# VectorE adds its half of a row one step sooner, and a seventh row buffer, in a mixture-of-experts and transformer kernel on one core

## The chip, the cores and the metric

The kernel runs on one core of a Trainium2 chip. The metric is the device time of one launch in microseconds. Three timed runs of the kernel before gave 3349.99, 3354.9 and 3366.16 us, median 3354.9. The engines are TensorE (PE, its weight loads PEld), VectorE (DVE), ScalarE (ACT), GpSimd (POOL) and SyncE (SP), which only issues transfers.

## What is computed

512 tokens of width 1024 in fp32 go through two blocks. The part that matters here is the end of the first block, a feed-forward layer that picks for every token 128 of 16384 experts (8 heads, 16 each), and the second block, which follows it:

```python
best, pos = lax.top_k(cand.reshape(...), 16)
gate = jax.nn.softmax(best, axis=-1)
ue = jnp.take(expert_u, expert, axis=0)
ve = jnp.take(expert_v, expert, axis=0)
h = jax.nn.gelu(jnp.einsum('thkd,td->thk', ue, xc))
out = jnp.einsum('thk,thkd->td', gate * h, ve)
```

Then come a final norm and the second block: differential attention, an MLP with squared ReLU (width 4096), multi-head latent attention (MLA), the same MLP with other weights, and a norm.

## The kernel before, in words

Each engine runs one long program in the order in which its instructions were written, and waits on semaphores for the others.

**Rows.** The tokens are four tiles of 128. For tile tt and choice k there is one "row", n = 128 tt + k, so 512 rows. For row n GpSimd issues one indirect transfer (`pool_rows`, L1708) that brings for each of the 128 tokens the 2048 values (u and v) of its k-th expert into a row buffer of 128 x 2048 values. VectorE then takes the dot product of the u half with the normed tokens (`dve_dot`, L1826). ScalarE makes from it the row's weight (`act_weight`: gelu L1776, times the gate L1778) and a diagonal matrix of the weights (L1783). The v half times the weight is added up in PSUM. For rows 0 to 255 TensorE does this for all 1024 columns, by a matmul with the diagonal (`pe_rows`, L1727). For rows 256 to 511 (`both_add`) TensorE adds columns 0 to 511 and VectorE adds columns 512 to 1023 (`dve_rows`, L1808; the first row of a tile L1805). The row buffer is free when both have added.

**Buffers.** `row_of(n)` gives the buffer of row n. Rows below 236 use ten buffers, later rows six (numbers 4 to 9: two in `un`, four in `raw`), since the others' place is taken by split weights of the tail. `row_before(n)` is the row that had the buffer before, and the gather of row n waits for the adds of that row. The normed tokens lie in `XN`, four tiles of 1024 columns. From row 256 on the dot product reads them from PSUM instead, where ScalarE copies tile 2 at step 255 and tile 3 at step 383 (L1757). `sums` are two places for the finished sum of a tile (`act_join`, L1792); sums[1] is filled at row 255, read by the transposes right after, and next filled at row 511.

**Steps.** All engines go through rows by steps. At step s VectorE does dot(s+1) and then the add of `late(s)`, which is s below 256 and s-1 (`LAG` = 1) from 256 on; ScalarE makes the weight of s+1; TensorE adds `late(s)`.

**The tail beside the rows.** The tail is the second block, and it runs for each half of the tokens. Steps 256 to 512 run beside the tail of the first half: `with_rows` and `beside` put 1.1 steps (`RATE`) after each unit of tail work, in the same places on every engine. The second half's tail then runs alone. The tail's weights come from HBM in tiles of 512 KB that SyncE loads (`sp_load`, L283), four raw places in turn. ScalarE rounds a tile to a high part (`act_hi`, L292), GpSimd subtracts it to get the low part (`pool_lo`, L298), and TensorE works with both.

**GpSimd's order.** GpSimd has gathers and splits to do. `self.spot` holds the place on TensorE, counted in turns, at which a row is added or a weight tile is used last. Before the gather of row n, `pool_rows` puts all the splits whose place came free on TensorE no later than the buffer of row n did. So the distance of six rows sets both what a gather waits for and where it stands among the splits.

The functions touched are `peer_tiles` (from L1363), `row_of`, `pool_rows`, `act_rows` and `dve_rows`.

Of the kernel before, what the change touches and what calls it, by code (L numbers as in the profile page):

```python
# [18 lines left out]
NBANK = 8  # L19
FEW_ROWS = 236  # L20
RATE = 1.1
LAG = 1
COLS = 53120
A_U = 5504
# [2 lines left out]
A_W2 = A_RAW + 8192  # L27
A_T = A_W2 + 8192
A_G = A_T + 8192
A_GEL = A_G + 4096  # L30
# [157 lines left out]
class Net:  # L188
# [1174 lines left out]
    def peer_tiles(self):  # L1363
        U, scr = 4096, self.scr
# [24 lines left out]
        self.modw = self.raw[0:4]  # L1389
        un = self.un  # L1390
        self.rows = [self.w01[:, 2048 * i:2048 * i + 2048] for i in range(4)] + [un[:, 0:2048], un[:, 2048:4096]] + self.raw[0:4]
        self.chosen = [un[:, 4096 + 128 * i:4224 + 128 * i].bitcast(U32) for i in range(4)]
        self.gate = [un[:, 4608 + 128 * i:4736 + 128 * i] for i in range(4)]
        self.dots, self.gelus, self.weight = (un[:, 5120 + 128 * i:5248 + 128 * i] for i in range(3))
# [4 lines left out]
    @staticmethod  # L1399
    def row_of(n):  # L1400

        return n % 10 if n < FEW_ROWS else 4 + (n - FEW_ROWS) % 6

    def row_before(self, n):

# [281 lines left out]
    def pool_rows(self, e):  # L1687
        S = "peer_pool"
        lows = [k for k in self.keys if len(k) == 3]
        at = 0  # L1690
        for n in range(512):
            tt, k, r = n // 128, n % 128, self.row_of(n)
            before = self.row_before(n)
            while n >= FEW_ROWS + 12 and at < len(lows) and self.spot_before(lows[at]) <= self.spot.get(("row", before), 0):
                self.pool_lo(e, lows[at])
                at += 1
            if k == 0:
                e.wait_ge(*self.at("peer_dve", ("expert", tt)))
            if before is not None:
                e.wait_ge(*self.at("peer_pe", ("acc", before)))  # L1700
                if self.both_add(before):
                    e.wait_ge(*self.at("peer_dve", ("acc", before)))
            elif r == 0:
                e.wait_ge(*self.at("peer_pe", ("xn", 3, 1)))
            elif r == 6:
                e.wait_ge(*self.at("peer_pe", "mod20"))
            index = bass.IndirectOffsetOnAxis(ap=self.chosen[tt][:, k:k + 1], axis=0)
            e.indirect_dma_start(self.rows[r], None, self.d["peer_uv"], index).then_inc(*self.tick(f"row{r}", n, 16))  # L1708
        for key in lows[at:]:
            self.pool_lo(e, key)  # L1710
# [39 lines left out]
    def act_rows(self, e):  # L1750
        S, D_, P_ = "peer_act", "peer_dve", "peer_pe"
        for n in range(-1, 512 + LAG):
            if n in (255, 383):
                e.wait_ge(*self.at(D_, ("dot", n)))
                if n == 255:
                    e.wait_ge(*self.at(S, ("sums", 0)))
                e.copy(self.xn_bank(), self.XN[:, n // 128 + 1, :]).then_inc(*self.tick(S, ("xn", n // 128 + 1)))  # L1757
            if n + 1 < 512:
                self.act_weight(e, n + 1)
            if self.late(n) in (127, 255, 383, 511):  # L1760
# [32 lines left out]

    def dve_rows(self, e):
        S, A_, P_ = "peer_dve", "peer_act", "peer_pe"
        for step in range(-1, 512 + LAG):
            if step + 1 < 512:
                self.dve_dot(e, step + 1)
            n = self.late(step)
            if n is not None and self.both_add(n):  # L1800
                v, w, acc = self.rows[self.row_of(n)][:, 1536:2048], self.weight[:, n % 128:n % 128 + 1], self.ps[:, 7, :]
                e.wait_ge(*self.at(A_, ("weight", n)))
                if n % 128 == 0:
# [2 lines left out]
                else:  # L1806
                    e.wait_ge(*self.at(S, ("acc", n - 1)))
                    e.scalar_tensor_tensor(out=acc, in0=v, scalar=w, in1=acc, op0=ALU.mult,  # L1808
                                           op1=ALU.add).then_inc(*self.tick(S, ("acc", n)))
            if step in (130, 386 + LAG):  # L1810
                for j in range(8):
                    self.dve_join(e, step // 128 - 1, j)
            yield

    def dve_dot(self, e, n):
# [1239 lines left out]
```

## Time and profile before

| | us |
|---|---|
| median of 3 timed runs | 3354.9 (3349.99 to 3366.16) |
| profiled execution | 3351.66 |
| its span, first to last instruction | 3349.8 |
| TensorE busy | 2778.6 (83%) |
| VectorE busy | 1978.0 (59%) |
| GpSimd busy | 1667.0 (50%) |
| ScalarE busy | 1433.5 (43%) |
| gathers' transfers, share of the 16 DMA engines | 39.8% |

The first block's other parts take until about 760 us. The rows of the first two tiles follow until about 1440 us, with the gathers as the main load. Rows 256 to 511 run with the tail of the first half until about 2550 us, and the second half's tail runs to the end. A busy share over the whole span mixes these. A table by stretches of time shows for each engine its busy time there, the TensorE clock that was granted (1 is 2.4 GHz), the share of the DMA engines and the bytes moved. A table of waits names for each group of instructions the engine or transfer that came last before they could start.

### The profile page before, as it was taken

The numbers are of one execution on the slowest core, as the hardware profiler recorded it, in microseconds if no ns is written. First come the engines' busy times: TensorE is split into PE (matmuls) and PEld (weight loads), VectorE is DVE, ScalarE is ACT, GpSimd is POOL, SyncE is SP. The second block draws the span as 40 slices with busy tenths as digits, with TensorE's granted clock in tenths as the row PEclk, the third lists the DMA queues.
The fourth block names the chain that finished last, engine by engine and source line by source line (L and its number), as shares of the span: only waits on it lengthen the run. The fifth ranks groups of instructions, "written<-read, shape, count | busy, mean of one in ns | idle before, by whom it ended". The sixth has DMA issues, their size and how long they took to land.

```text
span 3349.8 us, 43400 instructions
## 1 busy us (share of the span) xinstructions
PE 2778.6 (83%) x15438; PEld 2137.0 (64%) x15438; DVE 1978.0 (59%) x4260; ACT 1433.5 (43%) x3189; POOL 1667.0 (50%) x1014
## 2 busy tenths in 40 slices
PE   6987997787788787779778987678887989988898
PEld 4846996562333332266467766457776968987898
DVE  5785444466776766676765657666666464245423
ACT  2222222223333333356845445675444344444543
POOL 3812222254444443446257765447774607863575
PEclk8988998898999999888789998889998989988999
DMA  7210001219999999779669997888995404642364
GB/s 286 90 62 1 1 1 51 115 49 405 421 421 421 421 421 421 309 306 383 242 246 354 380 360 275 349 301 336 382 369 224 153 1 146 190 139 75 113 177 126
DMA packets 140518, 797.49 MB, mean 238 GB/s; under 512 B 15504, under 2 KB 18704, under 8 KB 67600
## 3 DMA queue, kind: packets, MB, share of 16 engines
q0 software_dynamic: 73728, 536.90, 39.8%
q1 hardware_dynamic: 65856, 253.36, 22.0%
q10 hardware_dynamic: 720, 4.46, 0.3%
q8 instruction: 124, 2.03, 0.2%
q14 instruction: 90, 0.74, 0.1%
HBM read 788.10 MB, written 6.55 MB: 237 GB/s over the span
## 4 chain that ended last, share of the span: by engine, by line
PE 45%; DMA 14%; DVE 11%; issue 10%; POOL 9%; ACT 5%; ACTq 0%; DVEq 0%; POOLq 0%; SPq 0%
PE ps L1727 7%; PE ps L2435 6%; DMA raw<-in_peer_uv,un 6%; PE ps L1925 6%; PE ps L870 6%; PE ps L2456 6%; DMA w<-in_peer_uv,un 5%; PE ps L328 4%; POOL wls L298 3%; POOL wlw L298 3%; DMA un<-in_peer_uv,un 2%; POOL raw L1708 2%; DVE scratch L1826 2%; PE ps L2122 2%; DVE gel L1985 1%
## 5 line engine op out<-in xcount | busy, mean ns | idle before, releaser
L298 POOL TENSOR_TENSOR wls<-raws,whs 128x1024 fp32r<-128x1024 f32 (+1 forms) x256 | 610.4, 2394 | 423.2 <-ACT whs L292 420.9
L1727 PE MATMUL ps<-raw,un 128*128 128x512 f32 x760 | 405.7, 650 | 109.1 <-ACT un L1783 106.8
L1708 POOL DMA_INDIRECT raw<-in_peer_uv,un x276 | 283.6, 1027 | 311.6 <-PE ps L1727 153.7
L1776 ACT ACTIVATE un<-un 128x1 f32<-128x1 f32 x512 | 103.7, 202 | 717.7 <-DVE scratch L1826 681.0
L1925 PE MATMUL ps<-ts,whs 128*128 128x256 f32 x1424 | 303.4, 314 | 25.0 <-DVE ts L1994 21.5
L298 POOL TENSOR_TENSOR wlw<-raws,whw 128x1024 fp32r<-128x1024 f32 x112 | 267.6, 2404 | 109.6 <-ACT whw L292 109.3
L292 ACT CAST whs<-raws 128x1024 fp32r<-128x1024 f32 (+1 forms) x256 | 263.8, 1036 | 87.3 <-PE ps L2456 35.4
L1727 PEld LDWEIGHTS ps<-raw,un 128*128 128x128 f32 x760 | 137.3, 203 | 253.9 <-ACT un L1783 173.6
L1826 DVE SCALAR_TENSOR_TENSOR scratch<-raw,ps 128x1024 f32<-128x1024 f32 x172 | 209.4, 1217 | 149.7 <-DMA raw<-in_peer_uv,un 145.3
L1925 PEld LDWEIGHTS ps<-ts,whs 128*128 128x128 f32 x1424 | 242.5, 206 | 56.6 <-issue 34.2
L1727 PE MATMUL ps<-w,un 128*128 128x512 f32 x384 | 201.7, 670 | 89.2 <-ACT un L1783 89.2
L1727 PE MATMUL ps<-un 128*128 128x512 f32 x392 | 209.7, 647 | 53.9 <-ACT un L1783 53.7
L2456 PE MATMUL ps<-ts,whs 128*128 128x256 f32 x1216 | 244.6, 302 | 3.2 <-DVE ts L2509 3.2
L1783 ACT ACTIVATE un<-kept,un 128x128 f32<-128x128 f32 x512 | 205.7, 402 | 48.5 <-ACT un L1778 1.5
L1708 POOL DMA_INDIRECT un<-in_peer_uv,un x140 | 136.9, 978 | 164.8 <-PE ps L1727 82.4
L2435 PE MATMUL ps<-ts,whw 128*128 128x256 f32 x960 | 196.0, 305 | 24.7 <-DVE ts L1994 21.7
L2456 PEld LDWEIGHTS ps<-ts,whs 128*128 128x128 f32 x1216 | 196.5, 195 | 25.6 <-issue 20.7
L1925 PE MATMUL ps<-ts,wls 128*128 128x256 f32 x712 | 210.2, 295 | 0.0
L2435 PE MATMUL ps<-ts,whs 128*128 128x256 f32 x1088 | 209.2, 293 | 0.0
L1727 PEld LDWEIGHTS ps<-w,un 128*128 128x128 f32 x384 | 75.9, 210 | 208.6 <-ACT un L1783 137.8
L298 POOL TENSOR_TENSOR wl<-raw,wh 128x2048 fp32r<-128x2048 f32 x23 | 106.9, 4656 | 201.9 <-ACT wh L292 201.9
L1708 POOL DMA_INDIRECT w<-in_peer_uv,un x96 | 102.8, 1070 | 176.9 <-PE ps L1727 152.6
(426 smaller groups left out, 7069.9 us busy)
## 6 DMA issues: line engine op xcount, KB each, us to landing
raws<-in_w_up SPq DMA_DIRECT2D x128, 512.0 KB
raws<-in_w_down SPq DMA_DIRECT2D x128, 512.0 KB
raws<-in_w_qk SPq DMA_DIRECT2D x32, 512.0 KB
scratch<-in_ada_w SPq DMA_DIRECT2D x13, 1024.0 KB, 14.3
raw<-in_w_in SPq DMA_DIRECT2D x11, 1024.0 KB, 5.9
raw<-in_ada_w SPq DMA_DIRECT2D x11, 1024.0 KB, 4.8
raw<-in_peer_w_q SPq DMA_DIRECT2D x8, 1024.0 KB, 7.0
raws<-in_w_v SPq DMA_DIRECT2D x16, 512.0 KB
```

Of the source, the lines that this page charges most:

```text
L292: e.copy(self.wh[h][:, 0:width], self.raw[slot][:, 0:width]).then_inc(*self.tick("hi", key))
L298: e.tensor_tensor(self.wl[h][:, 0:width], self.raw[slot][:, 0:width], self.wh[h][:, 0:width].bitcast(F32), ALU.subtract).then_inc(*self.ti ...
L328: ins = e.matmul(self.ps[:, b, :], l, r, start=k == 0 and i == 0, stop=k == nk - 1 and i == 2)
L870: ins = e.matmul(self.ps[:, b, 128 * q:128 * q + 128], l, r, start=n == 0, stop=n == len(terms) - 1)
L1708: e.indirect_dma_start(self.rows[r], None, self.d["peer_uv"], index).then_inc(*self.tick(f"row{r}", n, 16))
L1727: ins = e.matmul(self.ps[:, b + half, :], self.diag[n % 4], self.rows[self.row_of(n)][:, 1024 + 512 * half:1536 + 512 * half], start=k == ...
L1776: e.activation(self.gelus[:, c], self.dots[:, c], ACT.Gelu, bias=0.0, scale=1.0).then_inc(*self.tick(S))
L1783: e.activation(self.diag[n % 4], self.C("ident"), ACT.Identity, bias=0.0, scale=self.weight[:, c]).then_inc(*self.tick(S, ("diag", n)))
L1826: e.scalar_tensor_tensor(out=self.junk[n % 2 if n < 256 else 1], in0=self.rows[r][:, 0:1024], scalar=1.0, in1=xn, op0=ALU.mult, op1=ALU.mu ...
L1925: ins = e.matmul(o[:, 0:256], l, r, start=k == 0 and i == 0, stop=k == nk - 1 and i == 2)
L2435: ins = e.matmul(o[:, 0:256], l, r, start=k == 0 and n == 0, stop=k == 7 and n == 2)
L2456: ins = e.matmul(o[:, 0:256], l, r, start=t == 0 and n == 0, stop=t == 3 and n == 2)
```

## The change

The change does four things. First, VectorE's loop no longer lags: at step n it does dot(n+1) and then adds row n, not row n-1. TensorE still adds `late(n)`. Second, from row 278 (`SEVEN_ROWS`) on there are seven row buffers; the new one, number 10, is the place of tiles 2 and 3 of `XN`. Third, since that place is needed, ScalarE copies tile 3 of the normed tokens to sums[1] at step 270, after the transposes that read sums[1], and copies it from there to PSUM at step 383. Fourth, the first gather into buffer 10 (row 284) waits for that move.

```diff
--- before.py
+++ after.py
@@ -19,6 +19,7 @@
 NBANK = 8
 FEW_ROWS = 236
 RATE = 1.1
+SEVEN_ROWS = 278
 LAG = 1
 COLS = 53120
 A_U = 5504
@@ -1389,6 +1390,7 @@
         self.modw = self.raw[0:4]
         un = self.un
         self.rows = [self.w01[:, 2048 * i:2048 * i + 2048] for i in range(4)] + [un[:, 0:2048], un[:, 2048:4096]] + self.raw[0:4]
+        self.rows.append(scr[:, A_G - A_W2 + 2048:A_GEL - A_W2])
         self.chosen = [un[:, 4096 + 128 * i:4224 + 128 * i].bitcast(U32) for i in range(4)]
         self.gate = [un[:, 4608 + 128 * i:4736 + 128 * i] for i in range(4)]
         self.dots, self.gelus, self.weight = (un[:, 5120 + 128 * i:5248 + 128 * i] for i in range(3))
@@ -1399,7 +1401,10 @@
     @staticmethod
     def row_of(n):
 
-        return n % 10 if n < FEW_ROWS else 4 + (n - FEW_ROWS) % 6
+
+        if n < FEW_ROWS:
+            return n % 10
+        return 4 + (n - FEW_ROWS) % 6 if n < SEVEN_ROWS else 4 + (n - SEVEN_ROWS) % 7
 
     def row_before(self, n):
 
@@ -1700,6 +1705,8 @@
                 e.wait_ge(*self.at("peer_pe", ("acc", before)))
                 if self.both_add(before):
                     e.wait_ge(*self.at("peer_dve", ("acc", before)))
+            elif r == 10:
+                e.wait_ge(*self.at("peer_act", "xn moved"))
             elif r == 0:
                 e.wait_ge(*self.at("peer_pe", ("xn", 3, 1)))
             elif r == 6:
@@ -1754,7 +1761,12 @@
                 e.wait_ge(*self.at(D_, ("dot", n)))
                 if n == 255:
                     e.wait_ge(*self.at(S, ("sums", 0)))
-                e.copy(self.xn_bank(), self.XN[:, n // 128 + 1, :]).then_inc(*self.tick(S, ("xn", n // 128 + 1)))
+                    e.copy(self.xn_bank(), self.XN[:, 2, :]).then_inc(*self.tick(S, ("xn", 2)))
+                else:
+                    e.copy(self.xn_bank(), self.sums[1]).then_inc(*self.tick(S, ("xn", 3)))
+            if n == SEVEN_ROWS - 8:
+                e.wait_ge(*self.at(P_, ("join", 1, 1)))
+                e.copy(self.sums[1], self.XN[:, 3, :]).then_inc(*self.tick(S, "xn moved"))
             if n + 1 < 512:
                 self.act_weight(e, n + 1)
             if self.late(n) in (127, 255, 383, 511):
@@ -1793,11 +1805,10 @@
 
     def dve_rows(self, e):
         S, A_, P_ = "peer_dve", "peer_act", "peer_pe"
-        for step in range(-1, 512 + LAG):
-            if step + 1 < 512:
-                self.dve_dot(e, step + 1)
-            n = self.late(step)
-            if n is not None and self.both_add(n):
+        for n in range(-1, 512 + LAG):
+            if n + 1 < 512:
+                self.dve_dot(e, n + 1)
+            if 0 <= n < 512 and self.both_add(n):
                 v, w, acc = self.rows[self.row_of(n)][:, 1536:2048], self.weight[:, n % 128:n % 128 + 1], self.ps[:, 7, :]
                 e.wait_ge(*self.at(A_, ("weight", n)))
                 if n % 128 == 0:
@@ -1807,9 +1818,9 @@
                     e.wait_ge(*self.at(S, ("acc", n - 1)))
                     e.scalar_tensor_tensor(out=acc, in0=v, scalar=w, in1=acc, op0=ALU.mult,
                                            op1=ALU.add).then_inc(*self.tick(S, ("acc", n)))
-            if step in (130, 386 + LAG):
+            if n in (130, 386 + LAG):
                 for j in range(8):
-                    self.dve_join(e, step // 128 - 1, j)
+                    self.dve_join(e, n // 128 - 1, j)
             yield
 
     def dve_dot(self, e, n):
```

## Rows read from the trace of the kernel before

**Rows 1.** VectorE's adds, from their line's view; then stretches of time.
```profile
L1808 DVE SCALAR_TENSOR_TENSOR ps<-raw,un,ps x170: 743/751/755, 1446.9 to 2548.6; 128x512 f32<-128x512 f32 x170
...
core 0: us, PE busy (x) PEld busy (x) DVE busy (x) ACT busy (x) POOL busy (x), PEclk, DMA share, GB/s
1530.00:1590.00 60.00, 54.79 (x257) 36.55 (x257) 39.26 (x92) 39.80 (x90) 34.12 (x24) 0.83 0.96 386
1740.00:2036.00 296.00, 261.87 (x1681) 218.77 (x1679) 180.42 (x354) 148.98 (x347) 205.68 (x127) 0.97 0.88 343
2036.00:2290.00 254.00, 184.50 (x897) 134.84 (x898) 177.63 (x368) 166.55 (x371) 126.89 (x91) 0.85 0.85 322
2290.00:2545.00 255.00, 227.52 (x1474) 190.89 (x1472) 153.10 (x297) 127.61 (x298) 189.37 (x116) 0.97 0.93 361
```

**Rows 2.** Waits, 1740 to 2036 us: who for whom, total, times, longest.
```profile
DVE scratch L1826 <- DMA raw<-in_peer_uv,un: 61.5, 35, 4.9
...
DVE scratch L1826 <- DMA un<-in_peer_uv,un: 39.9, 20, 3.7
...
PE ps L1727 <- ACT un L1783: 28.0, 21, 3.0
```

**Rows 3.** Waits, 2290 to 2548 us.
```profile
DVE scratch L1826 <- DMA raw<-in_peer_uv,un: 61.8, 37, 4.4
DVE scratch L1826 <- DMA un<-in_peer_uv,un: 34.5, 18, 3.9
...
PE ps L1727 <- ACT un L1783: 16.7, 18, 3.4
```

**Rows 4.** Timeline of GpSimd in the first MLP: start, duration, instruction, idle before.
```profile
1786.84 2.40 POOL L298 TENSOR_TENSOR wlw<-raws,whw 128x1024 fp32r<-128x1024 f32 x1 [5.91 <-ACT whw L292]
...
1816.21 0.96 POOL L1708 DMA_INDIRECT raw<-in_peer_uv,un  x1
1817.86 0.94 POOL L1708 DMA_INDIRECT raw<-in_peer_uv,un  x1 [0.68 <-issue]
1825.55 2.39 POOL L298 TENSOR_TENSOR wlw<-raws,whw 128x1024 fp32r<-128x1024 f32 x1 [6.75 <-ACT whw L292]
1828.10 0.96 POOL L1708 DMA_INDIRECT un<-in_peer_uv,un  x1 [0.16 <-issue]
...
2010.83 2.41 POOL L298 TENSOR_TENSOR wlw<-raws,whw 128x1024 fp32r<-128x1024 f32 x1 [6.77 <-ACT whw L292]
```

**Rows 5.** DMA view, 1815 to 1851 us, in 40 slots of 0.9 us.
```profile
GB/s 414 414 428 432 419 414 410 419 451 432 437 382 137 0 0 86 218 455 423 428 369 410 150 309 341 296 423 437 423 428 391 460 446 428 391 405 405 432 423 419
```

**Rows 6.** The stretches' table, 1000 to 1100 us, gathers alone.
```profile
1000.00:1100.00 100.00, 79.38 (x183) 31.77 (x181) 71.35 (x217) 35.45 (x116) 44.25 (x41) 0.96 1.01 421
```

**Rows 7.** Waits, 2036 to 2290 us.
```profile
POOL raw L1708 <- DVE ps L1808: 48.1, 15, 4.7
...
PE ps L1727 <- ACT un L1783: 19.9, 11, 2.9
```

**Rows 8.** Timeline, a weight and the next dot product, in MLP and attention.
```profile
1862.02 0.29 ACT L1778 ACTIVATE un<-un 128x1 f32<-128x1 f32 x1
1863.01 1.22 DVE L1826 SCALAR_TENSOR_TENSOR scratch<-un,ps 128x1024 f32<-128x1024 f32 x1
...
2149.79 1.21 DVE L1826 SCALAR_TENSOR_TENSOR scratch<-un,ps 128x1024 f32<-128x1024 f32 x1
...
2153.31 0.30 ACT L1778 ACTIVATE un<-un 128x1 f32<-128x1 f32 x1
```

**Rows 9.** Timeline of ScalarE at row 384.
```profile
2008.81 0.99 ACT L1792 COPY un<-ps 128x1024 f32<-128x1024 f32 x1
```

**Rows 10.** Timeline, a weight load and the cast that needs it.
```profile
1831.53 0.33 SPq L283 DMA_DIRECT2D raws<-in_w_up  x1
...
1837.82 1.05 ACT L292 CAST whw<-raws 128x1024 fp32r<-128x1024 f32 x1
```

## The prediction

> **What bounds the kernel now.** I read the table by stretches first, because the change touches only rows 256 to 511, which share the time from about 1440 to 2550 us with the tail of the first half of the tokens (VectorE's adds start from 1446.9 to 2548.6 us [rows 1]). In it, look at the last columns. In the two MLP stretches [rows 1] TensorE is busy 261.9 of 296 us and 227.5 of 255 us, and the DMA share is 0.88 and 0.93. In the MLA stretch, 2036 to 2290 us, TensorE is at 184.5 of 254 us and DMA at 0.85. No engine is full in any of them, so something waits in a circle, and the next view is who waits for whom.
>
> Look at the MLP stretches: everybody waits for a row that has not landed. VectorE's dot product stands still for a gather 61.5 + 39.9 us in the first [rows 2] and 61.8 + 34.5 us in the second [rows 3]; TensorE waits 28.0 and 16.7 us for the diagonal that follows from that dot product [rows 2, 3]. The question is why the gather is late. It is not for want of a free buffer: GpSimd has no wait of note there for either accumulation. It is GpSimd's order. In its timeline [rows 4] it issues two gathers at 1816.21 and 1817.86, then reaches a split of weights whose high part ScalarE has not made, stands 6.75 us, and issues the next gather at 1828.10. The same stall is seen from 1786.84 to 2010.83 us in each of six spacings of (2010.83 - 1786.84) / 6 = 37.3 us, one group of the MLP (eight weight tiles). What it does to the DMA engines is in the rates of 0.9 us slots from 1815 us [rows 5]: some 420 GB/s before, then 137, 0, 0, 86, 218, then 455. With weights and gathers both held up behind that split, the DMA engines run dry once per group; otherwise they are full. The gathers alone, without weights, run at 421 GB/s [rows 6].
>
> **In the MLA stretch** the picture is another one. GpSimd waits there for VectorE's accumulation, 48.1 us for the raw buffers alone [rows 7], but VectorE's dot products hardly wait for rows; the attention's own round trips set the pace. An earlier gather is worth little there.
>
> **The change part by part.** The sum is made against the profiled execution, 3351.7 us with a span of 3349.8; the median of the three timed runs is 3354.9, which is 3.2 above it.
>
> *Seventh buffer: depth and order.* Row 278 is the first of seven. Each gather now waits for the accumulation seven rows back, not six. And since GpSimd's order is laid out by the place on TensorE at which that earlier row is used, each gather also moves one row ahead in the order, past about one weight split. In the stretch shown, the gather of 1828.10 would stand before the split that stalls until 1825.55, and be issued near 1818.8. So one more gather fills the dip of each group. GpSimd gets no added instruction; a split that the gather passes starts up to 0.96 us later [rows 4], and where it stalls, not at all. It is 128 x 8192 bytes = 1.05 MB, 2.49 us at 421 GB/s [rows 6]. The MLP stretches hold (296 + 255) / 37.3 = 14.8, say 15 groups: 15 x 2.49 = 37.4 us. Two ceilings on it from other rows: the DMA engines' unused time in these stretches, 296 x 0.12 + 255 x 0.07 = 53.4 us [rows 1], and TensorE's waits for the diagonal, 28.0 + 16.7 = 44.7 us [rows 2, 3]. 37.4 is under both; I keep it.
>
> *The same in the other stretches.* From 1530 to 1590 us the DMA share is 0.96 [rows 1], 2.4 us unused: I take 1, between 0 and 2.4. In the MLA stretch TensorE waits 19.9 us for the diagonal [rows 7], mostly behind VectorE's own attention work: I take 2, between 0 and 19.9.
>
> *VectorE's accumulation one step sooner.* The same instructions in a new order: no busy time is added. Before, step n did dot(n+1) then add(n-1); now it does dot(n+1) then add(n), which needs the weight of row n. In the MLP that weight ends at 1862.02 + 0.29 = 1862.31, and dot(n+1) ends at 1864.2 [rows 8], so the add does not wait. Setting every row's weight against the end of the next dot product over rows 257 to 510, it was later in 4 of 254, by 4.1 us in all; the worst is in attention, where the weight ends at 2153.61 and the dot product at 2151.0 [rows 8]. Cost: 0 to 4.1 us, taken as 0, as that engine's waits in attention cover it. Its gain: where GpSimd waits for VectorE's add (attention), the gather goes out a step sooner, onto DMA engines that are not what is late; taken as nothing beyond the 2 above. In the MLP GpSimd does not wait for the add, so alone this part is worth nothing there. On VectorE's queue the add moves past one dot product and past the piece of the tail between two steps; nothing else moves.
>
> *Moved and added on ScalarE.* One copy of 128x1024 at row 270 that was not there. A copy of this size took 0.99 us [rows 9]. ScalarE waits for a dot product at every row in this stage and the transposes it waits for are done long before; 0 to 1 us, taken as 0. The copy at 383 has another source and the same size. The gather of row 284 waits for the copy of step 270; fourteen rows lie between.
>
> *Row 384.* VectorE's add of row 384 moves ahead of dot(386), and it waits for ScalarE's copy of the sums, which runs from 2008.81 to 2009.80 [rows 9]. VectorE would come there about 2 us too early, once, and dot(386) is queued behind it: +2, between 0 and 4.
>
> *Weights against gathers.* The gather that fills the dip stands in front of weight loads. One load is issued at 1831.53 and cast by ScalarE at 1837.82, 6.3 us later [rows 10]; some two loads of a group have as little room. If they land 2.49 us later, ScalarE stands in order, and row weights are queued behind it. From both sides: 0, or 15 x 2 x 2.49 = 75 us if all of it reached TensorE. I take 3, near the lower end, because ScalarE's waits for a weight load are too small in both MLP stretches to be among the rows of note and it idles before nearly every row.
>
> The sum: 3351.7 - 37.4 - 1 - 2 + 2 + 3 = 3316.3 in terms of the profiled execution; against the median, which lies up to 3.2 higher, 3318.
>
> A rule of the Trainium skill speaks against this gain. First the row: gathers alone moved 421 GB/s for 100 us [rows 6], and the MLP stretches move 343 and 361 [rows 1]. The page "DMA: Bandwidth & Descriptors", section "Where 436 GB/s comes from", says that for transfers between HBM and SBUF the HBM side binds at about 358 GB/s per core. By it the MLP stretches would be at their ceiling and the time would stay near 3352. The trace disagrees, with 421 GB/s held for 100 us.
>
> **The rivals.**
> *The queue only gets longer (chance 0.19).* If the DMA engines' real ceiling with two kinds of traffic is near the share they have, an earlier gather lands no earlier. For: slots at full share around the dip vary from 150 to 455 GB/s [rows 5], so mixed traffic is less even than gathers alone. Against: the slots with 0. It would give back at most what the share leaves in the second stretch, 255 x 0.07 = 17.9 us with nothing from the first, less the 5 of costs: about 3339, and down to no change.
> *More than the dip (0.05).* If the circle of waits opens, TensorE's waits for the diagonal go altogether: 44.7 + 19.9 = 64.6 us, 3287.
> *Slower (0.08).* Later weight loads hold ScalarE, which holds the rows' weights, and TensorE waits for both. Price 75 us at the full rate; less the 37.4 it is 3351.7 + 38 = about 3390. It decides when more than half of those delays reach TensorE (2.49 x 30 x 0.5 = 37.4). Against it: 6.3 us is the tightest case I saw, and a load of half a gather's size has to land in that.
> *It does not do what it says.* Possible only if GpSimd's order stayed as it is and only the wait changed; then the MLP keeps its stall and only the MLA stretch gains, 0 to 4 us: counted with the first rival.
>
> **How the numbers follow.** The forecast has 0.68, the rivals as above. What a measurement of this kernel can tell from no change is about 0.5%, 16.8 us: under 3338 is faster, over 3372 slower. Faster: 0.68 + 0.05 = 0.73; same 0.19; slower 0.08. The forecast's own range is 3300 (the DMA ceiling in place of 37.4: 3351.7 - 53.4 - 3 + 5) to 3338; to hold 8 in 10 it is widened to 3296 and, for part of the first rival, to 3349.
>
> **What would show it.** In the profile after: the 37.3 us between once-a-group stalls down to about 34.8; VectorE's waits for rows in the MLP stretches down from 198 us to under 100; DMA share there up to about 0.97; VectorE's last add some 35 us before 2548.6; the second half's tail as long as before. GpSimd should wait for VectorE's add hardly at all, and for TensorE's more. The prediction is wrong if the DMA share rises but the groups stay as long (first rival), or if ScalarE's casts wait for weight loads (the slower case).

## The result, and the profile after

The changed kernel takes 3293.4 us (median; 3289.4 to 3296.3) against 3353.8 for the kernel before in the same series: a ratio of 0.9819, 95% interval 0.9803 to 0.9835, 60 us faster. Of all the executions in this document only two, both of the first experiment's kernel, stood apart, at 5362 and 5486 us; the ratios leave them out. The profiled execution is the fastest one, 3289.4 us with a span of 3287.6, so the two profiles differ by 62.2 us of span. The forecast was 3318 with 3296 as its lower end: the direction was right, the gain was about 1.7 times the 36 us that the forecast stands for, and the time lies just under the range.

Where the 62 us went is read by row numbers, not by equal times, since the later rows now come earlier. I divide both traces at VectorE's dot products of rows 320, 392, 448 and 511: a stretch of the first MLP, the MLA stretch, and one of the second MLP. First the table by stretches of the kernel after, its last line being the second half of the tokens, where no rows are gathered:

```profile
core 0: us, PE busy (x) PEld busy (x) DVE busy (x) ACT busy (x) POOL busy (x), PEclk, DMA share, GB/s
1734.00:2014.50 280.50, 258.84 (x1722) 218.71 (x1720) 195.14 (x378) 157.50 (x367) 215.51 (x133) 0.98 0.94 378
2014.50:2245.30 230.80, 171.29 (x839) 124.05 (x840) 166.38 (x349) 156.94 (x351) 118.75 (x86) 0.88 0.89 340
2245.30:2483.40 238.10, 228.70 (x1527) 193.82 (x1525) 160.15 (x310) 133.68 (x311) 193.04 (x117) 0.99 0.97 392
2540.00:3287.00 747.00, 680.68 (x5149) 654.58 (x5147) 313.60 (x745) 329.66 (x599) 423.90 (x178) 0.94 0.41 125
```

The same rows in the kernel before, divided at the same dot products (the stretches of [rows 1] are of the same kind, divided at round times):

```profile
1731.40:2043.60 312.20, 269.10 (x1723) 224.68 (x1723) 191.90 (x378) 157.07 (x367) 215.67 (x133) 0.96 0.89 346
2043.60:2279.80 236.20, 174.28 (x841) 126.22 (x840) 166.71 (x348) 157.44 (x352) 118.08 (x85) 0.86 0.86 322
2279.80:2544.70 264.90, 235.94 (x1524) 198.11 (x1524) 159.71 (x310) 133.78 (x311) 194.14 (x118) 0.97 0.92 357
2602.00:3349.70 747.70, 681.27 (x5143) 655.40 (x5141) 312.12 (x742) 329.50 (x599) 424.31 (x178) 0.94 0.41 124
```

The reader should see three things. The MLP stretches lose 31.7 and 26.8 us, 58.5 together; the MLA stretch loses 5.4; the second half is unchanged (row 320 itself comes 2.6 us later than before). The numbers of matmuls, splits and casts agree to within a few, so the same work is done. How well one such length repeats is shown by the twelfth experiment below, whose kernel differs from the changed one only in the second half: its three stretches took 281.9, 230.5 and 239.9 us, so a difference of under 2 us between single profiles says nothing. And TensorE gained twice: its idle time fell from 43.1 to 21.7 us and from 29.0 to 9.4 (41.0 together), and its busy time for the same matmuls fell from 269.1 to 258.8 and from 235.9 to 228.7 (17.5 together), with a granted clock that rose from 0.96 and 0.97 to 0.98 and 0.99.

Who waits for whom after, in the first MLP stretch and then in the second (engine, tile and line, what it waits for: us, times, longest), to be set beside [rows 2, 3]:

```profile
DVE scratch L1837 <- DMA raw<-in_peer_uv,un: 40.1, 31, 2.4
POOL wls L299 <- ACT whs L293: 27.2, 11, 12.9
POOL wlw L299 <- ACT whw L293: 24.0, 9, 6.1
...
DVE scratch L1837 <- DMA un<-in_peer_uv,un: 16.1, 12, 2.2
...
PE ps L1734 <- ACT un L1795: 9.1, 12, 1.7
...
PE ps L1734 <- ACT un L1804: 5.4, 1, 5.4
```

```profile
DVE scratch L1837 <- DMA raw<-in_peer_uv,un: 35.2, 29, 2.2
...
DVE scratch L1837 <- DMA un<-in_peer_uv,un: 18.0, 15, 2.3
...
PE ps L1734 <- ACT un L1795: 4.1, 5, 1.2
```

(L1837 is the dot product, L1826 before; L1734 the accumulation, L1727 before; L1795 the diagonal, L1783 before; L1804 the copy of a finished sum, L1792 before; L299 the split, L298 before; L293 ScalarE's cast, L292 before.) TensorE's waits for the diagonal are down from 28.0 and 16.7 us to 9.1 and 4.1. GpSimd's waits for a cast are down too. In the kernel before they were, in the first stretch:

```profile
POOL wls L298 <- ACT whs L292: 44.1, 13, 12.5
...
POOL wlw L298 <- ACT whw L292: 34.5, 11, 6.8
```

That is 78.6 us, and 51.2 after; in the second stretch 59.7 became 35.9. GpSimd's order, from its timeline after (start, duration, instruction, idle before it), to be set beside [rows 4]:

```profile
1812.78 0.96 POOL L1715 DMA_INDIRECT raw<-in_peer_uv,un  x1 [0.16 <-issue]
1814.04 0.94 POOL L1715 DMA_INDIRECT raw<-in_peer_uv,un  x1 [0.30 <-issue]
1819.26 2.40 POOL L299 TENSOR_TENSOR wlw<-raws,whw 128x1024 fp32r<-128x1024 f32 x1 [4.28 <-ACT whw L293]
1821.80 0.96 POOL L1715 DMA_INDIRECT raw<-in_peer_uv,un  x1
...
1985.59 2.38 POOL L299 TENSOR_TENSOR wlw<-raws,whw 128x1024 fp32r<-128x1024 f32 x1 [6.06 <-ACT whw L293]
```

The gather of row 344, which the kernel before issued at 1828.10 behind the split that stalled 6.75 us, is here the one of 1814.04, ahead of that split, and the stall is 4.28 us. In the same timeline it comes at 1785.15 too, and from there to 1985.59 are six groups: (1985.59 - 1785.15) / 6 = 33.4 us each, where it was 37.3. (In two of the six the longest stall is now 2.44 us or less.) In the second stretch the spacing fell from 37.3 to 32.9 us. Taken for 15 groups, the 3.9 us make 58.5 us: about the whole gain of the MLP stretches. The DMA rates after, 1800 to 1836 us in slots of 0.9 us as in [rows 5], show what became of the dip:

```profile
GB/s 428 405 437 428 396 423 391 419 396 391 419 410 428 432 391 414 441 410 405 432 423 428 423 432 419 264 341 414 410 410 364 378 328 423 350 296 405 441 428 387
```

Before, the slots 137, 0, 0, 86, 218 lacked, against 420 GB/s, 283 + 420 + 420 + 334 + 202 = 1659 GB/s x 0.9 us = 1.49 MB, or 3.55 us of transfer at 421 GB/s. After, 264 and 341 lack 156 + 79 = 235 x 0.9 us = 0.21 MB, or 0.5 us. So 3.0 us were won in this dip, where the forecast put the 2.49 us of one gather.

### The profile page after: what moved, and what is told of

It is laid out like the page before. It is cut to its first block, busy times and chain, and to the rows that moved or that the text cites. A ratio compares the mean times of both kernels' runs of the same rounds, so it can differ in the third digit from the quotient of the medians.

```text
span 3287.6 us, 43400 instructions
## 1 busy us (share of the span) xinstructions
PE 2757.0 (84%) x15438; PEld 2124.9 (65%) x15438; DVE 1979.9 (60%) x4260; ACT 1434.6 (44%) x3190; POOL 1668.1 (51%) x1014
## 4 chain that ended last, share of the span: by engine, by line
PE 44%; DMA 14%; DVE 12%; issue 9%; POOL 9%; ACT 5%; DVEq 0%; ACTq 0%; SPq 0%; POOLq 0%
PE ps L1936 7%; DMA raw<-in_peer_uv,un 7%; PE ps L1734 7%; PE ps L2467 6%; PE ps L2446 6%; PE ps L871 6%; DMA w<-in_peer_uv,un 5%; PE ps L329 4%; POOL wls L299 4%; DVE scratch L1837 2%; POOL wlw L299 2%; POOL raw L1715 2%; DMA un<-in_peer_uv,un 2%; DVE gel L1996 1%; PE ps L2133 1%
## 5 line engine op out<-in xcount | busy, mean ns | idle before, releaser
L299 POOL TENSOR_TENSOR wls<-raws,whs 128x1024 fp32r<-128x1024 f32 (+1 forms) x256 | 610.3, 2394 | 401.0 <-ACT whs L293 399.2
L1734 PE MATMUL ps<-raw,un 128*128 128x512 f32 x714 | 366.7, 630 | 84.8 <-ACT un L1795 84.5
L1715 POOL DMA_INDIRECT raw<-in_peer_uv,un x253 | 260.9, 1031 | 269.1 <-PE ps L1734 167.5
L299 POOL TENSOR_TENSOR wlw<-raws,whw 128x1024 fp32r<-128x1024 f32 x112 | 267.7, 2404 | 94.4 <-ACT whw L293 93.9
L293 ACT CAST whs<-raws 128x1024 fp32r<-128x1024 f32 (+1 forms) x256 | 263.9, 1036 | 98.4 <-PE ps L2467 35.2
L1734 PE MATMUL ps<-w,un 128*128 128x512 f32 x384 | 201.7, 669 | 88.6 <-ACT un L1795 88.6
L1734 PEld LDWEIGHTS ps<-raw,un 128*128 128x128 f32 x714 | 126.7, 198 | 225.8 <-ACT un L1795 150.7
L1734 PE MATMUL ps<-un 128*128 128x512 f32 x372 | 202.6, 660 | 42.6 <-ACT un L1795 37.2
L1837 DVE SCALAR_TENSOR_TENSOR scratch<-raw,ps 128x1024 f32<-128x1024 f32 x149 | 181.3, 1217 | 92.5 <-DMA raw<-in_peer_uv,un 90.3
L1795 ACT ACTIVATE un<-kept,un 128x128 f32<-128x128 f32 x512 | 205.7, 402 | 49.4 <-ACT un L1790 2.6
L1734 PEld LDWEIGHTS ps<-w,un 128*128 128x128 f32 x384 | 76.1, 210 | 207.9 <-ACT un L1795 137.4
L299 POOL TENSOR_TENSOR wl<-raw,wh 128x2048 fp32r<-128x2048 f32 x23 | 107.0, 4656 | 201.8 <-ACT wh L293 201.8
L1715 POOL DMA_INDIRECT un<-in_peer_uv,un x130 | 129.0, 992 | 150.2 <-PE ps L1734 102.3
```

Source lines behind the costliest of these rows:

```text
L293: e.copy(self.wh[h][:, 0:width], self.raw[slot][:, 0:width]).then_inc(*self.tick("hi", key))
L299: e.tensor_tensor(self.wl[h][:, 0:width], self.raw[slot][:, 0:width], self.wh[h][:, 0:width].bitcast(F32), ALU.subtract).then_inc(*self.ti ...
L1734: ins = e.matmul(self.ps[:, b + half, :], self.diag[n % 4], self.rows[self.row_of(n)][:, 1024 + 512 * half:1536 + 512 * half], start=k == ...
L1795: e.activation(self.diag[n % 4], self.C("ident"), ACT.Identity, bias=0.0, scale=self.weight[:, c]).then_inc(*self.tick(S, ("diag", n)))
L1837: e.scalar_tensor_tensor(out=self.junk[n % 2 if n < 256 else 1], in0=self.rows[r][:, 0:1024], scalar=1.0, in1=xn, op0=ALU.mult, op1=ALU.mu ...
```

## The experiments

The theory to be tested: the gain is GpSimd's order, one gather earlier among the splits. Its rivals: the depth of the ring (seven buffers), VectorE's sooner addition, or the three only together. All kernels below are timed in alternation with the kernel before, whose median lay between 3352.6 and 3356.2 us. In nine of them `place` gives the row by whose place on TensorE a gather is put in GpSimd's order; waits stay as the buffers need them:

```
-  ... self.spot_before(lows[at]) <= self.spot.get(("row", before), 0):
+  ... self.spot_before(lows[at]) <= self.spot.get(("row", self.place(n, before)), 0):
+    def place(self, n, before):
+        return n - 7 if n >= 285 else n - 6 if n == 284 else before
```

(The three dots stand for the unchanged start of a line.) The kernel before has n-6 there by itself, the changed one n-7. "Order 8" below is the same edit with n-8, and so on.

**One part alone, and two without the third.** The first has VectorE's new order alone:

```
-SEVEN_ROWS = 278
+SEVEN_ROWS = 1000
-    e.copy(self.xn_bank(), self.sums[1]).then_inc(...)
+    e.copy(self.xn_bank(), self.XN[:, 3, :]).then_inc(...)
```

> Six buffers and GpSimd's order as before; only VectorE's add of row n moves ahead of dot(n+2). Order theory (the gain comes from gathers standing one row earlier among GpSimd's splits): the MLP stretches stay as they are, 0 to 5 us faster than before, from the MLA stretch. Depth theory (the gain comes from rows being released and held one step sooner): a part of the 60 us, 15 to 30 us, since the add is the same one step sooner.

The second has seven buffers and their order, with VectorE's rows in the order of the kernel before:

```
-        for n in range(-1, 512 + LAG):
+        for step in range(-1, 512 + LAG):
...
-            if 0 <= n < 512 and self.both_add(n):
+            n = self.late(step)
+            if n is not None and self.both_add(n):
```

> Seven buffers with VectorE's add left where it was. Order theory: nearly all of the gain, 52 to 60 us faster than before. Depth theory: 30 to 45 us.

The third is the first with `place` at n-7: six buffers, and the order of seven.

> Six buffers, VectorE's add sooner, but each gather from row 285 on stands among GpSimd's splits where the changed kernel has it, by the place of the row seven back; it waits for the row six back. Order theory: GpSimd reached a gather 6.6 us after VectorE's add on average in the MLP, so one row (4.1 us) earlier seldom meets a buffer in use: 40 to 58 us faster than before. Depth theory: the gather now waits for its buffer with the splits queued behind it, so within 10 us of before or slower.

The fourth is the changed kernel with `place` at n-6: seven buffers, and the order of six.

> Seven buffers, add sooner, but GpSimd's order as in the kernel before, by the row six back. Order theory: the stall in front of a gather stays, 0 to 8 us faster than before. Depth theory: 45 to 60 us faster.

Measured: VectorE's order alone 3354.2 us (3353.0 without the two that stood apart), ratio 0.9993 (0.9983 to 1.0004); seven buffers with their order 3297.2, 0.9822 (0.9803 to 0.9841); six buffers with the order of seven 3299.1, 0.9835 (0.9818 to 0.9851); seven buffers with the order of six 3352.6, 0.9995 (0.9983 to 1.0006). The separation is clean, and each of the four came as the order theory had said: whichever kernel has the order has nearly the whole gain (57 to 59 us), and the one that has everything but the order has none that is clear of noise. With seven buffers and the old order GpSimd still stands 6.44 us behind its split and issues the gather after it:

```profile
1817.88 0.96 POOL L1715 DMA_INDIRECT un<-in_peer_uv,un  x1 [0.15 <-DVE scratch L1841]
1819.14 0.94 POOL L1715 DMA_INDIRECT raw<-in_peer_uv,un  x1 [0.30 <-issue]
1826.51 2.40 POOL L299 TENSOR_TENSOR wlw<-raws,whw 128x1024 fp32r<-128x1024 f32 x1 [6.44 <-ACT whw L293]
1829.07 0.96 POOL L1715 DMA_INDIRECT raw<-in_peer_uv,un  x1 [0.16 <-PE ps L1738]
```

**The order alone, and further.** The eighth kernel is the one before, VectorE's order included, with only `place` at n-7. The fifth and sixth are the changed kernel with n-8 and n-9, the seventh is the third with n-8.

> The kernel before, with nothing changed but GpSimd's order by the row seven back: no seventh buffer, VectorE's add where it was. If the order is all: 3297 to 3303. If the add sooner is what makes room for the order with six buffers (the gather then waits for an add that comes after one more dot product): 10 to 30 us slower than 3299.

> The changed kernel, with each gather from row 285 on one row earlier still in GpSimd's order (place of the row eight back; it waits for the row seven back). If the dip per group is what is left to gain: 5 to 20 us faster than the changed kernel's 3293. If the DMA engines and ScalarE's waits for weight loads are the limit by now: within 5 us of it. If the wait for the buffer now holds back the splits behind it: slower than it.

> The same, two rows earlier than the changed kernel. The gather now reaches GpSimd before its buffer is free and the splits stand behind it: slower than the kernel with the order of eight, by 5 to 40 us; equal to it if GpSimd has the room.

> Six buffers, add sooner, the order of the row eight back while waiting for the row six back. If the seventh buffer buys the room for an earlier order: slower than the 3299 of the order of seven with six buffers by 5 to 30 us. If buffers do not matter, as fast as the same order with seven.

Measured: order 7 alone 3308.4 us, 0.9857 (0.9831 to 0.9883); seven buffers with order 8 3287.6, 0.9799 (0.9775 to 0.9823), with order 9 3302.6, 0.985 (0.9823 to 0.9877); six buffers with order 8 3309.2, 0.987 (0.9844 to 0.9896). The last three came as expected; order 7 alone, 9 us above the third kernel, fell between its two expectations. The stretches tell why more is not better (when row 320 comes, and the stretches' lengths, in us; DMA rate in GB/s; the last column is GpSimd's wait for a buffer in the MLA stretch, summed over all waits of its gathers in the timeline but those called issue):

| kernel | row 320 | MLP 1 | GB/s | MLA | MLP 2 | GB/s | GpSimd waits |
|---|---|---|---|---|---|---|---|
| before | 1731.4 | 312.2 | 346 | 236.2 | 264.9 | 357 | 102 |
| sooner add alone | 1733.0 | 309.7 | 349 | 233.1 | 263.2 | 359 | 90 |
| seven, sooner add, order 6 | 1732.2 | 310.9 | 348 | 230.8 | 265.4 | 355 | 80 |
| order 7 alone | 1737.7 | 280.2 | 382 | 246.4 | 239.5 | 393 | 123 |
| six, sooner add, order 7 | 1733.0 | 282.5 | 375 | 237.5 | 237.4 | 393 | 112 |
| seven, order 7, add as before | 1736.8 | 283.2 | 374 | 234.0 | 241.3 | 386 | 101 |
| after (seven, sooner add, order 7) | 1734.1 | 280.5 | 378 | 230.8 | 238.1 | 392 | 89 |
| six, sooner add, order 8 | 1737.5 | 277.1 | 386 | 248.0 | 234.6 | 399 | 127 |
| seven, order 8 | 1741.3 | 270.6 | 392 | 236.2 | 231.3 | 400 | 110 |
| seven, order 9 | 1741.1 | 273.5 | 391 | 247.9 | 231.4 | 401 | 127 |

In the MLP every kernel with an earlier order wins 24 to 42 us a stretch, whatever its buffers. In MLA, an earlier gather reaches GpSimd while its buffer is in use, and the splits stand behind that wait. Order 7 alone costs 10.2 us there; the sooner add takes 8.9 of it back and the seventh buffer another 6.7. Put in the other way round the shares are 12.4 for the seventh buffer and 3.2 for the sooner add, so they overlap. That is what these two parts do: next to nothing in the whole time by themselves, but they make room for the order. (In the whole time the room that the sooner add gives is not clear of noise: 0.9857 against 0.9835, with intervals that overlap; it is read from the stretches.) GpSimd's waits for VectorE's addition in MLA show how the sooner add does it. With order 7 alone:

```profile
POOL raw L1715 <- DVE ps L1824: 59.5, 20, 5.3
POOL un L1715 <- DVE ps L1824: 47.0, 12, 7.3
```

and with the sooner addition beside it, on the same six buffers:

```profile
POOL raw L1715 <- DVE ps L1823: 30.6, 11, 4.1
POOL un L1715 <- DVE ps L1823: 19.2, 6, 4.9
```

(Part of it turns into waits for TensorE's accumulation: 13.1 + 3.8 us become 33.2 + 18.6.)

Order 8 costs in one more place: with seven buffers row 320 comes 7.3 us later than with order 7, which with the 5.4 us in MLA takes most of the 16.7 us gained in the MLP stretches, and the two ratios (0.9799 and 0.9819) have intervals that overlap.

**Order 8 where it pays.** If the MLP gains by order 8 and MLA loses, each should be had alone. The ninth kernel has order 8 in the MLP stretches only, the tenth outside them only (both are the changed kernel otherwise), the eleventh goes the other way: the kernel before, with each gather one row later (n-5).

```
+        return n - 8 if 326 <= n < 388 or 452 <= n else before            (ninth)
+        return n - 8 if 285 <= n < 326 or 388 <= n < 452 else before      (tenth)
+        return n - 5 if n >= 285 else before                              (eleventh)
```

> The changed kernel, with the order of eight only for rows 326 to 387 and from 452 on, whose gathers are issued in the two MLP stretches. Stretch theory (an earlier place pays in the MLP, where GpSimd stalls on a split, and costs in attention, where GpSimd stands at a gather whose buffer is in use and the splits wait behind): MLP stretches as short as in the run with the order of eight everywhere (270.6 and 231.4 us, 16 us less than the changed kernel), start and MLA stretch as in the changed kernel; 3277 to 3282 in all. Rival (the stretches are tied: rows gained in one are given back in the next): 3285 to 3292.

> The other half: the order of eight only outside the MLP stretches. Stretch theory: 8 to 14 us slower than the changed kernel. Rival: within 3 us of it.

> The kernel before with each gather one row later in GpSimd's order (place of the row five back), nothing else. Order theory: the same effect the other way round, 40 to 80 us slower than before, all in the MLP stretches, with VectorE's waits for rows up by about 4 us a row. Rival (before was at the DMA engines' pace and the order only matters by what it adds): within 15 us of before.

Measured: in the MLP only 3281.6 us, 0.9789 (0.9769 to 0.981); outside only 3299.7, 0.9833 (0.9812 to 0.9855); one row later 3502.3, 1.0435 (1.0412 to 1.0458). The stretches of the ninth and, under it, the two MLP stretches of the eleventh:

```profile
1730.40:2002.60 272.20, 256.17 (x1721) 217.66 (x1720) 197.53 (x378) 156.49 (x367) 215.00 (x133) 0.99 0.96 389
2002.60:2236.10 233.50, 175.49 (x839) 127.94 (x840) 167.03 (x349) 157.03 (x351) 119.14 (x87) 0.85 0.88 338
2236.10:2468.30 232.20, 223.54 (x1501) 190.75 (x1499) 160.70 (x309) 132.71 (x311) 190.72 (x116) 0.98 0.99 399
```

```profile
1739.20:2135.20 396.00, 287.31 (x1716) 236.59 (x1714) 190.91 (x378) 157.26 (x367) 218.91 (x136) 0.90 0.73 275
...
2371.80:2700.40 328.60, 252.83 (x1525) 208.61 (x1524) 160.03 (x310) 133.58 (x311) 192.81 (x118) 0.89 0.76 290
```

The ninth has the lowest median of the study, 71 us under the kernel before, and it came as the theory of stages said, except that MLA took 2.7 us more than in the changed kernel. It was not timed in one series with the changed kernel, and the two intervals overlap (0.9769 to 0.981 and 0.9803 to 0.9835), but four of its five runs lie 3.6 us or more under the lowest of the other's four, 3289.4, and the fifth 0.4 us above it. Its dip is gone: no slot of 0.9 us between 1796 and 1832 us is under 382 GB/s. The tenth, expected 8 to 14 us above the changed kernel, came 6.3 us above it, and those two intervals overlap as well; its stretches of 280.9, 236.4 and 242.0 us show the MLA stretch 5.6 us longer. The eleventh, expected at 40 to 80 us, cost 150 us (3502.3 against 3352.6), nearly all of it in the MLP stretches: 396.0 - 312.2 and 328.6 - 264.9, 147.5 in sum. Here GpSimd's stall has grown from 6.75 to 9.75 us, and the gathers stand behind it:

```profile
1795.40 0.94 POOL L1715 DMA_INDIRECT un<-in_peer_uv,un  x1 [0.30 <-issue]
1806.08 2.42 POOL L299 TENSOR_TENSOR wlw<-raws,whw 128x1024 fp32r<-128x1024 f32 x1 [9.75 <-ACT whw L293]
1808.63 0.96 POOL L1715 DMA_INDIRECT raw<-in_peer_uv,un  x1
```

It now stalls at several splits of a group, where it stood long at one: 4.84, 3.22, 3.76 and 7.14 us follow in the next 50 us. Its waits for casts in the first stretch are twice those of the kernel before (163.4 us against 78.6), and TensorE's for the diagonal three times (28.0 before):

```profile
POOL wls L299 <- ACT whs L293: 105.2, 22, 14.9
...
PE ps L1738 <- ACT un L1799: 90.3, 35, 9.6
...
POOL wlw L299 <- ACT whw L293: 58.2, 12, 9.7
```

One place in the order is thus worth far more on the late side (147.5 us in the MLP stretches) than on the early side (57.4 there with order 7 alone, then some 17 for the second place, nothing for the third).

**What a wait of TensorE costs.** The stretches had 17.5 us less TensorE busy time for the same matmuls. The twelfth kernel is the changed one with a wait put into the second half's MLPs, where no rows run: after a tile of the up projection, TensorE waits for what ScalarE makes of that tile.

```
                     ins.then_inc(*self.tick(S, ("s", g, t)))
+                    if H.h and g:
+                        e.wait_ge(*self.at(A_, ("hi", g, t)))
```

> The changed kernel with 56 pauses of TensorE in the second half's two MLPs, where nothing else is limiting: after each weight tile of the up projection from the second group on, TensorE waits until ScalarE has made the high part of that tile's result. Nothing is left out. Each pause is expected at 1.5 to 2 us. Theory of the missed term (a matmul runs slower for some time after TensorE has stood): TensorE's busy time in these stretches rises with the same matmuls, by about 0.6 us a pause, 25 to 45 us in all, beside the pauses themselves. Rival: busy time stays within 5 us, and the kernel is longer by the pauses alone, 80 to 115 us.

Measured: 3380.4 us, ratio to the kernel before 1.007 (1.0049 to 1.009). First the changed kernel and this one in the table by stretches, each from the dot product of row 511 to its end, then the added waits:

```profile
2483.40:3287.60 804.20, 717.77 (x5353) 687.78 (x5351) 350.78 (x827) 352.62 (x647) 439.56 (x185) 0.92 0.42 127
2486.50:3382.50 896.00, 734.43 (x5353) 693.29 (x5351) 352.76 (x827) 352.38 (x647) 441.59 (x185) 0.93 0.36 114
```

```profile
PE ps L2446 <- ACT ts L2503: 55.8, 42, 1.3
...
PE ps L2469 <- ACT ts L2503: 18.6, 14, 1.3
```

56 pauses of 1.33 us are 74.4 us idle. This part grew by 896.0 - 804.2 = 91.8 us, and TensorE's busy time by 734.4 - 717.8 = 16.7 of it for as many matmuls, 0.30 us for each pause, with the granted clock no lower. In the matmuls of the two MLPs alone, where all the pauses are, it grew by 11.8 us, 0.21 for each. So in these two profiles a pause costs 0.2 to 0.3 us more than its length even where the clock does not move. That is neither what the theory said (25 to 45 us) nor its rival (under 5 us). A caution: the length of this part lies between 800 and 810 us in the other kernels of this document, so the sum is known to some 5 us, and the two medians differ by 87 us and not by 95. Of the changed kernel's 17.5 us, 23 fewer waits of TensorE of any kind (25 + 19 of over 0.3 us before, 12 + 9 after) x 0.2 to 0.3 give 5 to 7, and some 11 are left.

For those 11 the trace of the kernel before has a candidate. TensorE's timeline there, behind one of the longer waits for the diagonal (start, duration, instruction, idle before it), and the clock around it:

```profile
1839.21 1.02 PE L1727 MATMUL ps<-un 128*128 128x512 f32 x2
1842.25 2.07 PE L1727 MATMUL ps<-un 128*128 128x512 f32 x2 [2.02 <-ACT un L1783]
```

```profile
1842.00:1843.00 1.00, 0.75 (x1) 0.49 (x2) 0.46 (x2) 0.97 (x4) 1.00 (x2) 0.64 1.04 430
1843.00:1844.00 1.00, 1.00 (x3) 0.34 (x1) 0.00 (x0) 0.89 (x1) 1.00 (x1) 0.50 1.05 442
1844.00:1845.00 1.00, 1.00 (x6) 0.89 (x5) 0.87 (x1) 0.00 (x0) 0.84 (x2) 0.50 1.04 438
1845.00:1846.00 1.00, 1.00 (x7) 1.00 (x7) 1.00 (x3) 0.50 (x2) 0.99 (x2) 0.65 0.93 389
1846.00:1847.00 1.00, 1.00 (x11) 1.00 (x10) 0.03 (x1) 0.40 (x1) 1.00 (x1) 1.00 1.00 410
```

After 2.02 us of idling the granted clock is 0.50, the 1.2 GHz level, for some three us, and the same pair of matmuls takes 2.07 us in place of 1.02. In the two MLP stretches before, a slow pair (1.44 to 2.07 us) follows five of the waits for the diagonal, of 2.02 to 2.47 us; after, one (2.08 us, behind the 5.4 us that TensorE waits for the copy of the sums at row 384). Behind the waits of 1 to 2 us it took 1.12 or 1.13. A slow pair does not follow every wait of that length: behind waits of 2.25, 2.98 and 3.44 us it took 1.12, 1.25 and 1.12. By the clock column the same share comes out: 269.1 x 0.96 against 258.8 x 0.98, and 235.9 x 0.97 against 228.7 x 0.99, leave 4.7 and 2.4 us, so about 10 of the 17.5 would be the clock and 7 the pauses, which fits (rough, since the clock is given in hundredths). This split was read, not tested by a kernel of its own.

## Why the prediction was right, and where it was wrong

**The bound and the mechanism: right.** GpSimd's order, with a gather behind a split that waits for its high part, was what held the MLP stretches. One reading of it was too even: I had the same stall in each of six groups, and in the third of them, between 1825.55 and 1896.11 us, the longest was 2.89 us. The order alone gives 46 of the 60 us (the eighth kernel), with the sooner add 57 (the third); moved the other way it costs 150.

**The first term, 37.4 us for the dip: mis-sized; the MLP stretches gave 58.5.** The number of groups, 15, was right, and the price of one was wrong: 2.49 us were put where the spacing fell by 3.9 (37.3 to 33.4, not the 34.8 forecast). This is the step of the forecast that failed: I had counted what one gather holds, not what the dip lacked. [rows 5] held the better number, 3.55 us of transfer missing in the dip, of which 3.0 came back. The stall of the split is itself shorter (6.75 to 4.28 us); that this is so because the circle through VectorE, ScalarE and TensorE closes sooner is argued, not shown. Other thin slots near it (150, 309, 341, 296 before; 364, 378, 328, 350, 296 after) lack 1.25 us of transfer before and 0.8 after, which brings the 3.0 to some 3.5 of the 3.9. I had taken the DMA engines to be full outside the dip and called the slot of 150 one of full share; the DMA view gives it a share of 0.6 only. 15 x 3.55 = 53 in the sum would have given about 3302.

**Both ceilings: wrong, and the one by the DMA share set the range's low end.** "TensorE's waits, 44.7" counted only one kind of wait of TensorE and only its idle time. All its idle time in the stretches fell by 41.0, and 17.5 us of busy time went with it (what each wait costs beyond its length, and a clock at 1.2 GHz behind some). "The DMA share's unused 53.4 us" took the share for a fixed quantity. Share x time in the two stretches was 0.89 x 312.2 + 0.92 x 264.9 = 521.6 us before and 0.94 x 280.5 + 0.97 x 238.1 = 494.6 after: 27 us less busy. The bytes differ little (rate x time gives 202.6 and 199.4 MB, 1.6% less), which accounts for some 8 of the 27; the rest is the same work in less busy time. Bytes against a rate that the trace shows held, 421 GB/s [rows 6], would have bounded it: 312.2 x (1 - 346/421) + 264.9 x (1 - 357/421) = 95.9 us. That ceiling holds, for the ninth kernel as well, whose MLP stretches are 72.7 us shorter than before, and I did not work it out.

**The Trainium skill's limit.** The second MLP stretch now moves 392 GB/s over 238 us, and up to 401 with order 9, in mixed traffic of gathers and weights. The page "DMA: Bandwidth & Descriptors", section "Where 436 GB/s comes from", has the HBM side bind at about 358 GB/s per core, a figure that it gets by halving a stack's 716 GB/s between two cores; the trace disagrees, as [rows 6] did already. All of this is with one core running.

**VectorE's addition one step sooner, and the seventh buffer's depth, at nothing: right** (0.9993 and 0.9995), with an interplay that I had not seen: both make room in MLA for the earlier order, 8.9 and 6.7 us as said above. MLA gained 5.4 where I took 2; seven buffers and the sooner add with the old order gain as much there (230.8), so in MLA it is the room itself. GpSimd's waits for VectorE's addition did not go, as I had forecast: 89.2 us in MLA before (48.1 + 41.1), 55.5 after. The engine's own attention work stands ahead of the addition in its program; that this is what keeps the 55.5 was not tested. Its waits for TensorE's accumulation rose as forecast, from 12.4 to 27.9 us.

**Row 384, 2 us: right for VectorE.** Its add of row 384 waits 2.1 us for ScalarE's copy of the sums, as said. TensorE waits for the same copy, 5.4 us where it waited 1.9. That is not this term: with the sooner add alone it is 2.3 us, and with seven buffers, order 7 and the add as before 5.3, so the longer wait goes with the order.

**Weights against gathers, 3 us: the wait came, the price hardly.** ScalarE's casts now wait 21 us for weight loads in the two stretches (1.7 before):

```profile
ACT whw L293 <- DMA raws<-in_w_up: 4.5, 4, 2.4
...
ACT whw L293 <- DMA raws<-in_w_up: 7.7, 6, 2.5
```

(first and second stretch, the largest group of each). But TensorE's idle time halved meanwhile, so at most a part of the 21 reached it. How much was not measured apart. The rival in which it decides did not come.

**The rivals.** "The queue only gets longer" fell: VectorE's waits for a landed row went down to 65.6 and 65.8 us (from 108.6 and 96.3), counting those for the new buffer, whose tile is called scratch, and the DMA share rose to 0.94 and 0.97, as said. (The forecast had these waits, 198 us in [rows 2, 3], under 100 for a gain of 37; a gain of 58 came with 131 left, for VectorE's wait is only a link of the circle.) VectorE's last addition came 62.8 us sooner (2485.8), not 35. "More than the dip", at 3287, was the case that came nearest, and 0.05 was too little for it: it had been read as the end of all of TensorE's waits for the diagonal, 64.6 us, but a gain of 60 came with 13.2 us of them left in the MLP stretches and 16.5 in MLA.

## What to carry to other kernels

On an in-order queue, ask of each instruction what it stands behind: a transfer issued behind a stalled operation is late however many buffers are free, and moving it by one place was worth some 50 us here, where one more buffer without that was worth none. Put a deeper ring and its order in separately, and choose the order by stage, since an early place pays where transfers are late and costs where buffers are. Size such a dip by the bytes that its slots lack, and bound the gain by bytes over the best rate that the trace shows, not by the unused share of time or by idle time alone.

## What the runs showed of the hardware that was not expected

- The DMA engines' busy share is not a measure of work: for bytes that differ by 1.6% share x time was 521.6 us while the stream had gaps and 494.6 after, and 401 GB/s went with a share of 0.99 where gathers alone moved 421 at 1.01.
- A pause of TensorE of 1.33 us came with 0.2 to 0.3 us more of busy time, with the granted clock no lower (56 pauses, one profile against one).
- After some idle times of 2 us and more the granted clock stood at 0.50 for about three us; after others of up to 3.44 us it did not. What decides between them stays open.
- The order one place later cost 150 us, about three times what one place earlier gave. GpSimd's stall grew from 6.75 to 9.75 us and came at several splits of a group. Of the 147.5 us in the MLP stretches 112.4 are TensorE's idle time and 35.1 its busy time (269.1 to 287.3 and 235.9 to 252.8), at a clock of 0.90 and 0.89 where it was 0.96 and 0.97; busy time x clock stayed the same in the first (258.3 and 258.6) and fell a little in the second (228.9 and 225.0), so the lower clock accounts for this growth. Why one place late is so much dearer than one place early stays open beyond this.
